# Expert weight blocks: four raw slots and four pairs of split slots in place of six and three

## The reference

```python
def swiglu_2(h, w_gate, w_up, w_down):
    return (jax.nn.silu(h @ w_gate) * (h @ w_up)) @ w_down
...
N_EXPERTS = 8
TOP_K = 2
D_FF_EXPERT = 1408
...
    return x + g_f * moe_swiglu(h, router_w, router_b, exp_gate, exp_up, exp_down)
```

## Time and profile before

| what | value |
|---|---|
| median of 3 runs | 2126.99 us (2125.64 to 2127.64) |
| the profiled execution | 2118.52 us |
| its span | 2116.7 us |
| PE busy | 1954.0 us (92%) |
| DVE busy | 1360.1 us (64%) |
| ACT busy | 999.9 us (47%) |
| DMA | 432.85 MB, mean 204 GB/s |

### The profile page before, as it was taken

The page is one execution under the profiler, slowest core; times in us unless marked ns, Lnnn a source line. Parts: engine busy times, 40 slices in busy tenths (PEclk is TensorE's granted clock), DMA queues, the critical chain, the costliest instruction groups (busy, mean ns, idle before and its releaser), DMA issues.

```text
span 2116.7 us, 24841 instructions
## 1 busy us (share of the span) xinstructions
PE 1954.0 (92%) x9699; PEld 1632.0 (77%) x9699; DVE 1360.1 (64%) x1855; ACT 999.9 (47%) x1371; POOL 71.1 (3%) x95
## 2 busy tenths in 40 slices
PE   6999899989997999998988999897889999999994
PEld 5888688868886878887876878786778888877773
DVE  4766766677666747666466754657544545588885
ACT  4434533354445644335445334435444434577774
POOL 1000000000000000000000100000000000000000
PEclk9999999999999999998998999898989999999997
DMA  8777477757772247775223785331095665699994
GB/s 288 231 244 243 146 239 239 236 195 231 245 244 69 99 168 235 242 239 159 72 90 102 252 296 187 107 91 59 11 321 179 215 197 201 218 358 366 361 358 146
DMA packets 302347, 432.85 MB, mean 204 GB/s; under 512 B 11987, under 2 KB 253974, under 8 KB 301974
## 3 DMA queue, kind: packets, MB, share of 16 engines
q1 hardware_dynamic: 282208, 356.65, 51.6%
q0 software_dynamic: 17824, 67.02, 9.4%
q10 hardware_dynamic: 2198, 7.59, 0.9%
HBM read 422.31 MB, written 14.68 MB: 206 GB/s over the span
## 4 chain that ended last, share of the span: by engine, by line
PE 73%; issue 11%; DVE 9%; ACT 6%; DMA 1%; ACTq 0%; POOLq 0%; POOL 0%; DVEq 0%; SPq 0%
PE acc L1857 9%; PE acc L1859 8%; PE acc L1858 8%; PE gate_bank L1857 7%; PE gate_bank L1858 6%; PE gate_bank L1859 6%; PE up_bank L1858 6%; PE up_bank L1859 6%; PE up_bank L1857 6%; DVE w_low L1212 3%; ACT w_high L731 2%; PE turn_bank L1970 1%; DMA raw<-in_e_ffn_up 1%; ACT probs L826 1%; DVE ada_sums L1271 1%
## 5 line engine op out<-in xcount | busy, mean ns | idle before, releaser
L1212 DVE TENSOR_TENSOR w_low<-raw,w_high 128x2048 fp32r<-128x2048 f32 (+2 forms) x372 | 779.0, 2100 | 454.0 <-ACT w_high L731 453.6
L731 ACT CAST w_high<-raw 128x2048 fp32r<-128x2048 f32 (+2 forms) x372 | 651.0, 1755 | 538.4 <-PE up_bank L1859 245.3
L1857 PE MATMUL acc<-w_high,hidden_high 128*128 128x512 f32 x682 | 272.8, 400 | 16.5 <-DVE hidden_low L1796 9.4
L1859 PE MATMUL acc<-w_high,hidden_low 128*128 128x512 f32 x682 | 267.6, 392 | 0.0
L1858 PE MATMUL acc<-w_low,hidden_high 128*128 128x512 f32 x682 | 266.8, 391 | 0.0
L1857 PE MATMUL gate_bank<-w_high,u_high 128*128 128x512 f32 (+1 forms) x604 | 240.2, 398 | 17.3 <-DVE w_low L1212 6.3
L1858 PE MATMUL gate_bank<-w_low,u_high 128*128 128x512 f32 (+1 forms) x604 | 233.1, 386 | 0.0
L1859 PE MATMUL gate_bank<-w_high,u_low 128*128 128x512 f32 (+1 forms) x604 | 233.0, 386 | 0.0
L1857 PE MATMUL up_bank<-w_high,u_high 128*128 128x512 f32 (+1 forms) x588 | 226.8, 386 | 0.0
L1858 PE MATMUL up_bank<-w_low,u_high 128*128 128x512 f32 (+1 forms) x588 | 226.4, 385 | 0.0
L1859 PE MATMUL up_bank<-w_high,u_low 128*128 128x512 f32 (+1 forms) x588 | 226.4, 385 | 0.0
(11 more groups left out here) (439 smaller groups left out, 2787.8 us busy)
## 6 DMA issues: line engine op xcount, KB each, us to landing
raw<-in_o_exp_gate SPq DMA_DIRECT2D x80, 512.0 KB, 5.3
raw<-in_o_exp_up SPq DMA_DIRECT2D x80, 512.0 KB, 6.9
raw<-in_o_exp_down SPq DMA_DIRECT2D x40, 1024.0 KB, 7.8
raw_ada<-in_e_ada_w POOLq DMA_DIRECT2D x24, 1024.0 KB, 5.8
raw_ada<-in_o_ada_w POOLq DMA_DIRECT2D x24, 1024.0 KB, 5.8
raw<-in_ffn_pre_wg SPq DMA_DIRECT2D x44, 512.0 KB, 6.0
raw<-in_ffn_pre_wu SPq DMA_DIRECT2D x44, 512.0 KB, 7.1
raw<-in_ffn_pre_wd SPq DMA_DIRECT2D x22, 1024.0 KB, 4.9
```

The costliest lines, as they stand in the source:

```text
L731: ins = nc.scalar.copy(dst(WH[c % RING]), src(RAW[RAW_SLOT[c]]))
L1212: ins = nc.vector.tensor_tensor(dst(WL[c % RING]), src(RAW[RAW_SLOT[c]]), dst(WH[c % RING]).bitcast(F32), ALU.subtract)
L1857: nc.tensor.matmul(to, sh, mh, start=first, stop=False, **kw)
L1859: return nc.tensor.matmul(to, sl, mh, start=False, stop=last, **kw)
```

## The change

The experts' stage gets four raw slots (one more than the rest of the kernel, not three more) and four pairs of split slots. The memory that the slots take stays the same: the places of two raw slots become `w_high3` and `w_low3`. Pairs are given out by new tables, `SPLIT_SLOT` and `SPLIT_BEFORE`, and ACT waits in `prep` for the block that last used the pair. In the experts' stage this is the block four before; in the rest of the kernel it is three before, as it was. The line that gives out raw slots is not edited; only `MOE_RING` in it is another number.

```diff
-MOE_RING = 6
+MOE_RING = 4
 RAW_SLOT, BEFORE = [], []
 for _c in range(N_BLOCKS):
     _j = _c - STREAM["moe"]
     RAW_SLOT.append(_c % RING if _j < 0 or _j % MOE_RING < RING else _j % MOE_RING)
     BEFORE.append(max((k for k in range(_c) if RAW_SLOT[k] == RAW_SLOT[_c]), default=None))
+SPLIT_SLOT, SPLIT_BEFORE = [], []
+for _c in range(N_BLOCKS):
+    SPLIT_SLOT.append(_c % RING if _c < STREAM["moe"] else (_c - STREAM["moe"]) % MOE_RING)
+    SPLIT_BEFORE.append(max((k for k in range(_c) if SPLIT_SLOT[k] == SPLIT_SLOT[_c]), default=-1))
...
             RAW += [sb(f"raw{s}", [P, BLOCK], into=stage) for s in range(RING, MOE_RING)]
+            WH += [sb(f"w_high{s}", [P, BLOCK], F32R, into=stage) for s in range(RING, MOE_RING)]
+            WL += [sb(f"w_low{s}", [P, BLOCK], F32R, into=stage) for s in range(RING, MOE_RING)]
...
                 act.wait_ge(raw_landed[RAW_SLOT[c]], LANDED[c])
-                hold(act, w_used, c - RING + 1)
+                hold(act, w_used, SPLIT_BEFORE[c] + 1)
                 for src, dst in moves:
-                    ins = nc.scalar.copy(dst(WH[c % RING]), src(RAW[RAW_SLOT[c]]))
+                    ins = nc.scalar.copy(dst(WH[SPLIT_SLOT[c]]), src(RAW[RAW_SLOT[c]]))
...
-                    ins = nc.vector.tensor_tensor(dst(WL[c % RING]), src(RAW[RAW_SLOT[c]]),
-                                                  dst(WH[c % RING]).bitcast(F32), ALU.subtract)
+                    ins = nc.vector.tensor_tensor(dst(WL[SPLIT_SLOT[c]]), src(RAW[RAW_SLOT[c]]),
+                                                  dst(WH[SPLIT_SLOT[c]]).bitcast(F32), ALU.subtract)
...
-                return [w[c % RING][:, 0:n].rearrange("p (k n) -> p k n", k=k) for w in (WH, WL)]
+                return [w[SPLIT_SLOT[c]][:, 0:n].rearrange("p (k n) -> p k n", k=k) for w in (WH, WL)]
```

More of the change, by code:

```diff
@@ L2095, in latent_queries @@
                 hold(pe, at_qr, p)
-                split = [w[c % RING] for w in (WH, WL)]
+                split = [w[SPLIT_SLOT[c]] for w in (WH, WL)]
                 for k in range(2):
```

## The result

The changed kernel took 2176.18 us (median, 2170.81 to 2178.19, 4 runs), the kernel before beside it 2126.88 us (2125.64 to 2127.64, 4 runs). The ratio is 1.0222, with a 95% interval of 1.0207 to 1.0238. That is 49.3 us slower, where I had forecast 16.5. The direction was right, and so was the loop of raw slots that sets the pace; its size was off by a factor of three, and the time lies above the range.

A forecast was written before the change was run, and what follows sets the result against it. PE and DMA were both taken as near their limits; with four slots the raw-slot loop would bind, 53.8 us per expert against 50.3. 4.72 experts x 3.5 = +16.5 us on 2127.0 gave 2143.5 us, range 2127 to 2160.

The forecast's parts named there:

- the loop of raw slots: One-chunk part of the experts' stage: waits for raw slots set the pace, 12.44 us for four blocks, +16.5 us in all.
- The place: Nothing changes up to 1835 us; the loss comes in the one-chunk part, over 85 blocks or 4.72 experts.
- the line of the table: L98 with 4 put in gives no ring; the raw slots' lead falls from six blocks to about three.
- the turn over four blocks: One-chunk part: 5.17 + 2.88 + 4.23 + 0.16 = 12.44 us for four blocks, two of them issued at once.
- ACT waiting for DMA in place of PE: One-chunk part: `w_high` often waits for DMA `raw`, not once as before.
- the rows: Token rows in and out delay the loop's transfers: 0 to 2.9 us per expert, taken as 1.4.
- ACT's waits in front of PE: One-chunk part: ACT's 44 us in front of PE shrink to a few.
- 5.17 + 2.88: Loading in a loop turn: 5.17 us from issue to landing of a lone block, 2.88 for the transfer queued behind it.
- the second loop of the other pair: Blocks m mod 4 = 0 and the 1 behind them close a loop of the same terms, 12.44 us.
- 3 x 1/4 x (1.91 + 2.29 - 1.05 - 1.22): Shorter splits of an expert's three half blocks, one pair of splits in four on the loop: 1.4 us back per expert.
- loads would land sooner: Faster rival: with fewer queued, a lone load takes 4.2 us and the fourth pair works as meant; some 2117 us, chance 0.07.
- The heavy rival: Slower by more: all disturbances fall on the loop, +28.8 us, and PE's clock falls; 2153 to 2165 us, chance 0.20.

The follow-up runs named there:

- the clean ring: The changed kernel with raw slots given out as m mod 4 in the experts' stage, four pairs kept: 2136.49 us, ratio 1.0038 to the kernel before.

## Why the prediction was off

**What held.** The place (nothing up to 1835 us beyond the difference between two executions, everything in the one-chunk part), the cause (the line of the table, 39.7 of the 49.3 us by the clean ring), the turn over four blocks with a pair issued at once, ACT waiting for DMA in place of PE, PE's small part in it (4.1 us at most for a third of its products there), and the rows (3 to 10 us against 6.6). That ACT's waits in front of PE would shrink held too, but mostly since the loads came late, and not by the fourth pair.

**The step that failed is the length of the loop's turn, above all its loading, "5.17 + 2.88", and in it the 5.17 us of the first block.** For whole blocks without rows or code the forecast had 8.05 us, and eight such turns took 9.15 in the mean: 6.32 us to the landing of the first block, not 5.17, and 2.83 from there to the landing of the second, as good as the 2.88. Over all 21 turns the loading was 1.36 us above the forecast, 28.6 us together. The 5.17 us came from a load that goes alone. In the changed kernel the first load of a turn seldom goes alone. In the three of the eight turns whose block before was at most 1.8 us from its landing the first block took 5.3 to 5.6 us; in the five where it was 2.4 to 3.6 us from it, 5.6 to 8.3. At 1912.91 the load of block 76 (issued 1909.62, landed 1914.72) was still on its way, and at 18 of the 21 starts of a turn the block before was 1.0 to 6.0 us from its landing. The prediction had seen the second loop of the other pair and had said that it closes with the same terms, but not that both share one DMA. Four whole blocks and 0.65 us of rows are 12.2 us of transfers at 364 GB/s in a turn of 12.44: DMA had to run without a gap, with a queue that is filled only when a split is done. It did not: its share was 0.89 and it moved 298 GB/s. Counted from the issues, landings and packets of the two traces, from the issue of m = 57 to that of m = 141:

| blocks in flight | changed kernel: us, GB/s | kernel before: us, GB/s |
|---|---|---|
| none or one | 62.0, 206 | 18.5, 208 |
| two | 130.7, 313 | 78.4, 345 |
| three | 84.5, 343 | 131.5, 365 |
| four | 10.2, 352 | 17.2, 367 |

In both kernels DMA moved less with fewer blocks in flight, and the changed kernel had at most two for 193 of its 287 us, the kernel before for 97 of its 246. Why two in flight moved less in the changed kernel (313 against 345) stays open. That the loading grows by 0.37 us per turn when the splits shrink by 1.86 fits this too: the loads of the other pair are then still further from their landings (3.2 us at the start of a turn in the mean, where it was 2.6). That the two loops disturb one another is my reading of the landings; no run took one of them away, and how much of it is PE's loads of code stays open.

**The second term that failed is the gain of half blocks, "3 x 1/4 x (1.91 + 2.29 - 1.05 - 1.22)".** It would have taken 0.31 us off a turn's splits. But only two of the 21 turns ended on a half block, and these gained 0.3 us each (3.97 and 3.93 us), as the split of a half block stood behind that of the block before it. Over 21 turns the splits are 7.3 us above the forecast, 0.7 of it in the first turn, where ACT and DVE came late. The fourth pair was put at nothing inside the loop and was worth some 7 us: with three pairs ACT still stood 15.8 us in front of PE. It acts the other way and does not explain the miss.

**The rivals.** That loads would land sooner is out: the quickest whole block of the one-chunk part took 4.84 us (m = 136), not 4.2. The Trainium skill, "DMA: Bandwidth & Descriptors", section "Anatomy of one DMA", had given that rival its 4.4 us for a MiB; the measurement decides against it here, with 9.15 us for a block and the one behind it, where an estimate by the page, which fits another queue, is 4.4 + 2.4. The heavy rival, disturbances on the loop and a falling clock, had the right sign with its bound of +28.8 us and was still too small. The clock did fall, from 1.00 to 0.95 in the mean of the part. It can't be what sets the pace: without a third of the products PE's clock was lower still (0.89 from 1845 to 2090 us), and the kernel was no slower (4.1 us less by the medians). The range was too narrow because every bound in it was on what meets the loop, and none on the price of a load, which I had taken from a state that the change removes.

## What to carry to other kernels

When a buffer is taken out of a ring, write out the table of who waits for whom with the new number, and compare the time from a slot's release to its next (load, wait in the queue, split) with the time in which the bound engine uses that many blocks. If the transfers fill nearly all of such a loop, the price of a lone load doesn't hold: put a range on it, up to the slowest landings that the trace shows. And ask of each kind of buffer who waits for it: here a fourth `w_high` beside five raw slots was worth 4.7 us (2127.13 to 2122.44). What a fourth `w_low` would add to that was not run; every kernel here that had one had four raw slots or three.

## What the runs showed of the hardware

Waits that are already met are not free on PE: 77 of them ahead of a gate-up held its weight loads 3.3 to 3.5 us (45.5 us in 14 places, 45.8 in 13), some 42 to 46 ns each. With a deep queue DMA held 366 GB/s over 48 us (the kernel before without the third products), and 298 GB/s over 290 us with a short one, the same loads in the same sizes. In the changed kernel the granted clock dropped eight times between 1867 and 2150 us to half, 2.4 to 1.2 GHz, for 3.4 to 6.8 us; one of them came at 1901.70, and in the 3.7 us before it PE was busy 0.20 us. From 1898 to 1904 us PE was busy 2.50 us, and the mean clock was 0.81:

```profile
1898.00:1904.00 6.00, 2.50 (x6) 1.97 (x7) 3.39 (x3) 3.05 (x4) 0.00 (x0) 0.81 0.82 269
```
